# One 512-column matmul in place of two of 260, token halves of 256 and 264, and the low weight products last

## The chip, the cores and the metric

The kernel runs on one core of a Trainium2 chip. The metric is the device time of one launch in microseconds; of the kernel before, three runs gave a median of 1429.27 us (1426.93 to 1429.67).

## The reference

Two layers of a decoder trunk, one inference step for 512 prompt tokens and 8 sample tokens that share all weights (520 tokens, model width 1024). What is computed, cut to the frame:

```
for layer in (0, 1):
    z = x @ w_in                              # even: 3592 columns, odd: 2236 columns
    y = mixer(z)                              # even: gated convolution + mLSTM; odd: NSA + DSA attention
    x = layer_norm(ALPHA * x + y @ w_out)
    x = layer_norm(ALPHA * x + square(relu(x @ w_up)) @ w_down)      # 1024 -> 4096 -> 1024
```

All values are float32. Nearly all arithmetic lies in the projections `x @ w`, and these are what the change touches.

## The kernel before, in words

Tokens lie along the free axis: `xT` is held as 8 blocks (k = 0..7) of 128 channels by 520 tokens. A "tile" g is one output block of 128 channels of a projection. There are 191 tiles: 29 of the even input projection (`G_IN0`), 8 of its output projection (`G_OUT0`), 64 of the first MLP (`G_MLP0`: four chunks of 8 up tiles and 8 down tiles), 18 of the odd input projection (`G_IN1`), 8 of its output (`G_OUT1`), 64 of the second MLP (`G_MLP1`).

Operands are split for accuracy: weights into a high part (`wr`, or a part of `ring_lo` in the even projection) and a low part (`ring_lo`), activations into a high part (`xh`, `hh`) and a low part (`xl`, `hl`). A tile is the sum over k of three products: high weight by high activation, high weight by low activation, low weight by high activation. Tokens are cut into two halves of 260 (`H2`), each accumulated in a PSUM bank of its own (`psA(g)`, `psB(g)`), so a tile takes 8 x 3 x 2 = 48 matmuls of 260 columns, all recorded at L1024 (`split_pass`). Two pairs of banks alternate between tiles (`banks_free` waits until the tile two before has been read out).

The order is written out by hand for every engine, with semaphores. Around the MLPs it is:

- PE: an up tile or down tile after the other (`split_tile`). The first 8 up tiles after a norm are a `head`: all 8 tiles over token half 0 first (a half tile of 24 matmuls each), then half 1 of the first four interleaved, then half 1 of the other four. This lets half 0 start while the other engines still norm half 1. The last tiles before a norm are a `tail`, with all half 0 before all half 1.
- ACT, in `hidden`: relu of half 0 out of PSUM (L1636, signals `free_a`), then the high part of the weights four tiles ahead (`w_hi_ahead`, L1599), then the square that makes `hh` (L1643).
- DVE, in `hidden`: relu of half 1 out of PSUM (L1996, signals `free_b`), the low part of the weights four tiles ahead (`w_lo_ahead`, L1972; it waits for the high part), then `hl` (L2001). Down tiles are added to `xT` by DVE, one operation for each half (`residual`, L1983 and L1984). In the head, DVE's and ACT's lists also hold the second half of the norm: DVE `normed` (L2051) and `x_low` (L2068, L2070), ACT `scaled` (L1670).
- POOL squares the relu (L842) and in the head subtracts the mean (`centre`, L808).

In the even input projection, ACT copies half 0 and DVE half 1 out of PSUM (L2291); DVE also runs the convolution and the sample heads there, and the sigmoid's reciprocal (L2310).

Of the kernel before, what the change touches and what calls it, by code (L numbers as in the profile page):

```python
# [27 lines left out]
P = 128  # L28
# [5 lines left out]
H2 = T // 2  # L34
# [43 lines left out]
def build(nc, x_prompt, x_sample, state_conv, state_C, state_n, state_m, cache_kv, cache_idx, cache_win, page_table,  # L78
# [20 lines left out]
    with ExitStack() as ctx:  # L99
# [11 lines left out]
        with ExitStack() as mixer:  # L111
            big = mixer.enter_context(nc.sbuf_tensor("big", [P, KF, T], F32))
            ymix = mixer.enter_context(nc.sbuf_tensor("ymix", [P, KD, T], F32))
            cbuf = mixer.enter_context(nc.sbuf_tensor("cbuf", [P, 4096], F32))
        with ExitStack() as odd:

            odd.enter_context(nc.sbuf_tensor("projections", [P, len(O_NAMES) * T], F32))
            xl1 = odd.enter_context(nc.sbuf_tensor("xl1", [P, KD, T], F32R))
            odd.enter_context(nc.sbuf_tensor("behind", [P, (KF - KD - len(O_NAMES)) * T], F32))
            xh1 = odd.enter_context(nc.sbuf_tensor("xh1", [P, KD, T], F32R))  # L120


        xh = sb("xh", [P, KD, T], F32R)
        xl = sb("xl", [P, KD, T], F32R)
        hh = sb("hh", [P, KD, T], F32R)
        hl = sb("hl", [P, KD, T], F32R)
# [12 lines left out]
        def piece(n):  # L139
# [13 lines left out]
            pn_ok dsd_ev pb_mm pb_ev pt_mm pt_ev kc_ok pc_mm vf_mm vf_ev pc_n pct_mm q_sc q_mm kv_out  # L153
# [248 lines left out]

        def cols(half):
            return slice(half * H2, (half + 1) * H2)

# [14 lines left out]
        def hid_event(c, j, half=None):  # L420

            return j + KD * half if c == 0 else KD * (c + 1) + j

# [87 lines left out]
        XL = {0: xl, 1: xl1, 2: xl}  # L511
        racc = att[:, 0:T]
# [220 lines left out]
        def _(pool):  # L733
# [98 lines left out]
            def hidden(layer, g, c, j, half=None):  # L832
# [3 lines left out]
                if half != 1:  # L836
                    pool.wait_ge(sm["free_a"], g + 1)
# [22 lines left out]
            for k in range(KD):  # L860
                if k not in XE_DVE:
                    pool.wait_ge(sm["tin_a"], k + 2)
                    pool.wait_ge(sm["tin_b"], 1)
                    pool.tensor_tensor(hl[:, k, :], xT[:, k, :], xh1[:, k, :].bitcast(F32), ALU.subtract).then_inc(sm["xe_p"], 1)
# [114 lines left out]
        def _(pe):  # L979
# [32 lines left out]
            def split_pass(gs, halves, hi, lo, ready_hi=None, ready_lo=None, between=None, ks=range(KD)):  # L1012

                for g in gs:
                    weights_here(g)
                for k in ks:
                    for part, ready, x in ((0, ready_hi, hi), (0, ready_lo, lo), (1, None, hi)):
                        if ready:
                            ready(k)
                        first, final = k == ks[0] and x is hi and part == 0, k == ks[-1] and part == 1  # L1020
                        for g in gs:
                            w = w_split(split_of[g])[part]
                            for half in halves:
                                last = pe.matmul(bank(g, half)[0:width(g), 0:H2], w[:, k, :], x[:, k, cols(half)],  # L1024
                                                 start=first, stop=final)
                                if final:
                                    half_done(last, half)
# [3 lines left out]
            def split_tile(g, hi, lo, ready=None, between=None):  # L1031

                banks_free(g)
                split_pass((g,), (0, 1), hi, lo, ready, between=between)
# [14 lines left out]
            def head(n_ln, g):  # L1049
# [10 lines left out]
                for i in range(n):  # L1060
                    if i >= 4:
                        pe.wait_ge(sm["free_a"], g + i - 3)
                    split_pass((g + i,), (0,), XH[n_ln], XL[n_ln], first_tile if i == 0 else None,
# [4 lines left out]
                split_pass(range(g, g + first), (1,), XH[n_ln], XL[n_ln], x_hi_here(n_ln, 1), x_lo_here(n_ln, 1))  # L1068
                for i in range(first, n):
                    if i >= 4:  # L1070
                        pe.wait_ge(sm["free_b"], g + i - 3)
                    split_pass((g + i,), (1,), XH[n_ln], XL[n_ln])

            def tail(n_ln, g, hi, lo, ready=None, ready_b=None, ks=range(KD)):

                for half in range(2):
                    for i in range(TAILS[g]):
                        if half == 0 and i < 2 and n_ln in (0, 2):
                            if i == 1:
                                pe.wait_ge(sm["free_a"], g - 1)  # L1080
                                pe.wait_ge(sm["free_b"], g - 1)
                                split_pass((g, g + 1), (0,), hi, lo, ready, ks=ks)
# [10 lines left out]
                        split_pass((g + i,), (half,), hi, lo, (ready, ready_b)[half] if i == 0 else None, ks=ks)  # L1093
# [31 lines left out]
            def mlp(layer, g):  # L1125

                for c in range(NFC):
                    if c == 0:
                        head(2 * layer, g)
                    else:  # L1130
                        for j in range(KD):
                            split_tile(g + j, xh, xl)
                    g += KD
                    if c < NFC - 1:
                        for j in range(KD):
                            split_tile(g + j, hh, hl, hidden_here(layer, c) if j == 0 else None)
                    else:
                        for j in range(KD - TAILS[TAIL_OF[layer]]):
                            split_tile(g + j, hh, hl, hidden_here(layer, c) if j == 0 else None)
                        tail(2 * layer + 1, TAIL_OF[layer], hh, hl, hidden_here(layer, c))  # L1140
                    g += KD

            def norm_sums(n_ln, half):
# [3 lines left out]
                mm(ps[4 * half][:, 0:H2], meanM[:, :], racc[:, cols(half)])  # L1147
                mm(ps[4 * half + 1][:, 0:H2], meanM[:, :], sacc[:, cols(half)]).then_inc(sm["stats_mm"], 1)
# [34 lines left out]
            split_pass((G_IN0,), (0, 1), xh1, hl, xe_here, xe_low_here)  # L1183
# [6 lines left out]
            for idx in range(len(E_TILE)):  # L1190
                if idx:
                    split_tile(G_IN0 + idx, xh1, hl)
# [5 lines left out]
                if idx == 2:  # L1198
# [4 lines left out]
                    for half in range(2):  # L1203
                        last = mm(ps[4 + half][0:4, 0:H2], ident[0:8, 4:8], gz[:, half * H2:(half + 1) * H2])
# [96 lines left out]
            tail(0, G_OUT0, xh, xl, y_even_here)  # L1301
# [8 lines left out]
            for idx, name in enumerate(O_NAMES):  # L1310
                if idx == 0:
                    head(1, G_IN1)
                if idx >= 4:
                    split_tile(G_IN1 + idx, xh1, xl1, between=selected if idx == 4 else None)
# [263 lines left out]
            tail(2, G_OUT1, xh, xl, y_odd_here(0), y_odd_here(1), Y_ODD)  # L1578
# [15 lines left out]
        def _(act):  # L1594
# [32 lines left out]
            def hidden(layer, g, c, j, half=None):  # L1627
# [3 lines left out]
                if half != 1:  # L1631
                    tile_done(g, 0)
# [3 lines left out]
                    act.activation(rel[j % 2][:, 0:H2], psA(g)[:, 0:H2], ACT.Relu).then_inc(sm["free_a"], 1)  # L1636
# [1102 lines left out]
```

## Time and profile before

| | |
|---|---|
| median of three runs | 1429.27 us |
| span of the profiled execution | 1421.2 us |
| what lies between the two (median less span) | 8.1 us |
| PE busy | 1366.7 us, 96% of the span |
| DVE / ACT / POOL busy | 52% / 36% / 28% |

The page gives the profiled execution as its span, from first to last instruction; it has no time of its own beside it, so the 8.1 us in the table also hold the difference between one execution and a median. In a timeline, the first two numbers of a row are start and duration in us; the duration of a matmul runs into that of the next ones, so that what one costs is read as the distance of starts. A float32 matmul that is not split stands in the trace as two records, a float32r matmul (L1024) as one.

### The profile page before, as it was taken

To read this page: it belongs to the slowest core of one execution; us is meant where nothing else is said; L and a number is where in the kernel's file an instruction comes from. 1 tells how busy PE (TensorE), PEld (TensorE's weight loads), DVE (VectorE), ACT (ScalarE), POOL (GpSimd) and SP (SyncE) were. 2 spreads that over 40 slices of the span, in tenths; PEclk is the share of its full clock that TensorE was granted. 3 is DMA by queue.
4 is the path that set the end of the run, shared out by engine and by line. 5 is a ranking of instruction groups with operands and counts; after the bars stand their busy time and mean duration, and the time that the engine had idled before them with its cause. 6 is when DMAs were issued, how large, how long until landed. Compare 5 with 4: busy or idle time off the path is not lost. (4 is left out here: it accounts for less than half of the span.)

```text
span 1421.2 us, 27641 instructions
## 1 busy us (share of the span) xinstructions
PE 1366.7 (96%) x11359; PEld 1287.3 (91%) x11359; DVE 745.3 (52%) x1378; ACT 504.6 (36%) x1004; POOL 397.1 (28%) x470
## 2 busy tenths in 40 slices
PE   6999998999999999999899999999999999999996
PEld 5999975899999999999899966667999999999996
DVE  3424777667434343343879856454774343343435
ACT  3321224345314023032542366786553032140311
POOL 3014423365101010014744473023652010010102
PEclk9999999999999999999999999999999999999998
DMA  5343170030323131312323226204113313132301
GB/s 156 125 114 107 43 238 6 3 119 31 126 83 117 63 119 60 119 60 52 60 90 60 64 82 216 61 2 120 64 56 120 119 60 119 60 119 69 110 31 60
DMA packets 87196, 123.86 MB, mean 87 GB/s; under 512 B 24438, under 2 KB 42302, under 8 KB 87040
## 3 DMA queue, kind: packets, MB, share of 16 engines
q1 hardware_dynamic: 82048, 107.00, 23.6%
q0 software_dynamic: 5024, 15.10, 3.6%
q8 instruction: 91, 1.49, 0.4%
q14 instruction: 33, 0.27, 0.1%
HBM read 115.62 MB, written 8.57 MB: 87 GB/s over the span
## 5 line engine op out<-in xcount | busy, mean ns | idle before, releaser
L1024 PE MATMUL ps<-xh,ring_lo 128*128 128x260 f32 (+2 forms) x2496 | 503.5, 283 | 1.4 <-ACT big L1599 1.4
L1024 PEld LDWEIGHTS ps<-xh,ring_lo 128*128 128x128 f32 (+2 forms) x2496 | 382.6, 187 | 3.3 <-ACT big L1599 2.3
L1024 PE MATMUL ps<-xl,wr 128*128 128x260 f32 x1568 | 351.4, 283 | 6.1 <-DVE xl L2070 3.9
L1024 PE MATMUL ps<-xh,wr 128*128 128x260 f32 x1568 | 352.9, 284 | 2.5 <-POOL xl L824 1.2
L1024 PEld LDWEIGHTS ps<-xl,wr 128*128 128x128 f32 x1568 | 255.2, 188 | 8.2 <-DVE xl L2070 5.1
L1024 PEld LDWEIGHTS ps<-xh,wr 128*128 128x128 f32 x1568 | 256.0, 188 | 5.0 <-ACT att L1636 1.4
L842 POOL TENSOR_TENSOR att<-att 128x520 f32<-128x520 f32 (+1 forms) x80 | 77.3, 967 | 548.6 <-DVE att L1996 521.5
L1972 DVE TENSOR_TENSOR ring_lo<-ring,wr 128x1024 fp32r<-128x1024 f32 (+1 forms) x144 | 192.1, 1337 | 62.1 <-ACT wr L1599 62.0
L1024 PE MATMUL ps<-hh,wr 128*128 128x260 f32 x1024 | 222.1, 283 | 0.0
L1024 PE MATMUL ps<-hh,ring_lo 128*128 128x260 f32 x1024 | 221.8, 283 | 0.0
L1024 PE MATMUL ps<-hl,wr 128*128 128x260 f32 x1024 | 221.7, 283 | 0.0
L1599 ACT ACTIVATE wr<-ring 128x1024 fp32r<-128x1024 f32 (+1 forms) x162 | 167.4, 1049 | 130.1 <-PE ps L1024 120.4
L1024 PEld LDWEIGHTS ps<-hh,wr 128*128 128x128 f32 x1024 | 164.5, 188 | 0.2 <-issue 0.2
L1024 PEld LDWEIGHTS ps<-hh,ring_lo 128*128 128x128 f32 x1024 | 164.5, 188 | 0.0
L1024 PEld LDWEIGHTS ps<-hl,wr 128*128 128x128 f32 x1024 | 164.0, 188 | 0.0
L1636 ACT ACTIVATE att<-ps 128x260 f32<-128x260 f32 x64 | 24.6, 384 | 304.4 <-PE ps L1024 304.4
L1983 DVE TENSOR_TENSOR xT<-xT,ps 128x260 f32<-128x260 f32 x96 | 37.5, 422 | 162.9 <-PE ps L1024 162.9
L1996 DVE TENSOR_SCALAR att<-ps 128x260 f32<-128x260 f32 x64 | 27.4, 428 | 137.4 <-PE ps L1024 137.4
L1024 PE MATMUL ps<-hl,ring_lo 128*128 128x260 f32 (+1 forms) x464 | 93.4, 283 | 0.0
L1599 ACT ACTIVATE big<-ps 128x260 f32<-128x260 f32 (+6 forms) x104 | 40.3, 402 | 148.5 <-PE ps L1024 133.2
L789 POOL TENSOR_TENSOR ring_lo<-ring,wr 128x1024 fp32r<-128x1024 f32 x18 | 43.3, 2412 | 109.8 <-ACT wr L1599 109.8
L986 PE MATMUL ps<-big 128*64 128x128 f32 (+3 forms) x504 | 66.7, 348 | 4.8 <-DVE small L2694 3.3
(354 smaller groups left out, 1620.8 us busy)
## 6 DMA issues: line engine op xcount, KB each, us to landing
ring<-in_w_up SPq DMA_DIRECT2D x16, 2048.0 KB, 7.9
ring<-in_w_down SPq DMA_DIRECT2D x16, 2048.0 KB, 7.9
ring<-in_w_in_e SPq DMA_DIRECT2D x9, 1024.0 KB, 5.6
ring<-in_w_in_e SPq DMA_DIRECT2D x2, 2048.0 KB, 8.8
ring<-in_w_out_e SPq DMA_DIRECT2D x2, 2048.0 KB, 8.8
ring<-in_w_in_o SPq DMA_DIRECT2D x16, 256.0 KB, 5.0
ring<-in_cache_kv POOLq DMA_DIRECT2D x32, 128.0 KB, 2.4
ring<-in_w_out_o SPq DMA_DIRECT2D x8, 512.0 KB, 8.9
```

What stands on the lines that cost most here:

```text
L789: pool.tensor_tensor(w_l, w_raw(u), w_h.bitcast(F32), ALU.subtract).then_inc(sm["w_lo_p"], 1)
L842: pool.tensor_tensor(hid[j % 2][:, cc], rel[j % 2][:, cc], rel[j % 2][:, cc], ALU.mult).then_inc(sm["hid_sq"], 1)
L986: return pe.matmul(out, lhsT, rhs, start=start, stop=stop, skip_group_check=True)
L1024: last = pe.matmul(bank(g, half)[0:width(g), 0:H2], w[:, k, :], x[:, k, cols(half)], start=first, stop=final)
L1599: return act.activation(out, in_, ACT.Copy, scale=scale)
L1636: act.activation(rel[j % 2][:, 0:H2], psA(g)[:, 0:H2], ACT.Relu).then_inc(sm["free_a"], 1)
L1972: dve.tensor_tensor(w_l, w_raw(u), w_h.bitcast(F32), ALU.subtract).then_inc(sm["w_lo"], 1)
L1983: last = (dve.tensor_tensor(x, x, y, ALU.add) if scale is None else dve.scalar_tensor_tensor(x, x, scale, y, ALU.mult, ALU.add))
L1996: dve.tensor_scalar(rel[j % 2][:, H2:T], psB(g)[:, 0:H2], 0.0, None, ALU.max).then_inc(sm["free_b"], 1)
```

## The change

Tokens are halved as 256 and 264. In most tiles (`apart`: all output and MLP tiles but the first tile of each MLP, and 23 of the 29 even input tiles; 165 tiles in all) the bank of half 0 is used as two regions of 256 columns. One matmul of 512 columns multiplies the high weights with the high and the low activations of half 0 at once (high activations into one region, low activations into the other); the low-weight product is added to the second region. Whoever reads half 0 out adds the two regions. To have high and low activations in one access pattern, they are put into one tensor (`x2`, `h2`, `x12`, `xe2`). Tiles that wait for nothing at their start (`low_last`) run all 8 k of the high weights first and wait for the low weights only then. DVE and ACT swap their halves in the even projection and in `hidden`.

```diff
+HALVES = (slice(0, 256), slice(256, T))
+HW = (256, T - 256)
...
+        def apart(g, half):
+            if half or g in (G_IN0, G_IN0 + GATE, G_MLP0, G_MLP1) or G_IN1 <= g < G_OUT1:
+                return False
+            return g >= G_OUT0 or not 16 <= E_TILE[g - G_IN0] < 20
...
+            def product(g, half, part, n, k, x, order, first, final):
+                hi, lo = order
+                w = w_split(split_of[g])[part][:, k, :]
+                m = HW[half]
+                region = bank(g, half)[0:width(g), :]
+                last = None
+                if not apart(g, half):
+                    last = pe.matmul(region[:, 0:m], w, x[:, n, k, cols(half)], start=first and n == hi, stop=final)
+                elif part:
+                    last = pe.matmul(region[:, m:2 * m], w, x[:, hi, k, cols(half)], start=False, stop=final)
+                elif n == lo:
+                    both = region.rearrange("p (n t) -> p n t", n=2)
+                    last = pe.matmul(both if hi == 0 else both[:, ::-1], w, x[:, :, k, cols(half)], start=first, stop=False)
+                if final:
+                    half_done(last, half)
...
+            def low_last(g, x, order, between=None):
+                pe.wait_ge(sm["w_hi"], split_of[g] + 1)
+                for k in range(KD):
+                    for n in order:
+                        for half in range(2):
+                            product(g, half, 0, n, k, x, order, k == 0, False)
...
+                weights_here(g)
+                for k in range(KD):
+                    for half in range(2):
+                        product(g, half, 1, order[0], k, x, order, False, k == KD - 1)
...
@@ ACT, hidden @@
-                if half != 1:
-                    tile_done(g, 0)
+                if half != 0:
+                    tile_done(g)
+                    act.wait_ge(sm["free_b"], g)
...
-                    act.activation(rel[j % 2][:, 0:H2], psA(g)[:, 0:H2], ACT.Relu).then_inc(sm["free_a"], 1)
+                    act.activation(rel[j % 2][:, cols(1)], psB(g)[:, 0:HW[1]], ACT.Relu).then_inc(sm["free_b"], 1)
+                if half != 1:
+                    act.wait_ge(sm["free_a"], g + 1)
+                    act.activation(rel[j % 2][:, cols(0)], rel[j % 2][:, cols(0)], ACT.Relu).then_inc(sm["rel_ok"], 1)
                 if g + 1 != TAIL_OF[1]:
                     w_hi_ahead(g, 1 if half is None else half)
...
@@ DVE @@
+                if apart(g0 + m, half):
+                    link(last)
+                    last = dve.tensor_tensor(x, x, bank(g0 + m, half)[:, HW[half]:2 * HW[half]], ALU.add)
...
+            def summed(out, g, n=P):
+                if apart(g, 0):
+                    return dve.tensor_reduce(out, psA(g)[0:n, :].rearrange("p (n t) -> p t n", n=2), AX.X, ALU.add)
+                return dve.tensor_copy(out, psA(g)[0:n, 0:HW[0]])
...
-                if half != 0:
-                    tile_done(g)
+                if half != 1:
+                    tile_done(g, 0)
...
-                    dve.tensor_scalar(rel[j % 2][:, H2:T], psB(g)[:, 0:H2], 0.0, None, ALU.max).then_inc(sm["free_b"], 1)
+                    summed(rel[j % 2][:, cols(0)], g).then_inc(sm["free_a"], 1)
                 if g + 1 != TAIL_OF[1]:
                     w_lo_ahead(g, 1 if half is None else half)
```

How the instructions of PE stand in an up tile of the steady part, before (one k, halves in banks `ps0` and `ps1`):

```order
L1024 MATMUL ps0<-xh,ring_lo 128x260
L1024 MATMUL ps1<-xh,ring_lo 128x260
L1024 MATMUL ps0<-xh,wr 128x260
L1024 MATMUL ps1<-xh,wr 128x260
L1024 MATMUL ps0<-xl,wr 128x260
L1024 MATMUL ps1<-xl,wr 128x260
```

and after:

```order
L1041 MATMUL ps0<-x2,wr 128x512
L1036 MATMUL ps1<-x2,wr 128x264 x2
L1041 MATMUL ps0<-x2,wr 128x512
L1036 MATMUL ps1<-x2,wr 128x264
L1038 MATMUL ps0<-x2,ring_lo 128x256
L1036 MATMUL ps1<-x2,ring_lo 128x264
L1038 MATMUL ps0<-x2,ring_lo 128x256
L1036 MATMUL ps1<-x2,ring_lo 128x264
```

(the last two k of the high weights and the first two of the low). Two matmuls of `ps0` in a k have become one; the low-weight products (`ring_lo`) have gone behind all eight k.

ACT at the start of the first MLP's head, before; L1636 is the relu out of PSUM, L1599 `wr<-ring` the high part of weights, L1643 the square:

```order
L1677 ACTIVATE att<-ps 128x260
L1636 ACTIVATE att<-ps 128x260 [waits mm_a]
L1599 ACTIVATE wr<-ring 128x1024 [waits mm_b,w_slot0]
L1643 ACTIVATE hh<-att 128x260 [waits free_a]
L1681 ACTIVATE att<-att 128x260 [waits std_in]
L1636 ACTIVATE att<-ps 128x260 [waits mm_a]
L1599 ACTIVATE wr<-ring 128x1024 [waits mm_b,w_slot0]
```

and after, with the relu at L1686 and the high part at L1645:

```order
L1727 ACTIVATE att<-ps 128x264
L1686 ACTIVATE att<-att 128x256 [waits free_a]
L1645 ACTIVATE wr<-ring 128x1024 [waits mm_b,w_slot0]
L1693 ACTIVATE h<-att 128x256 [waits rel_ok]
L1731 ACTIVATE att<-att 128x264 [waits std_in]
L1686 ACTIVATE att<-att 128x256 [waits free_a]
L1645 ACTIVATE wr<-ring 128x1024 [waits mm_b,w_slot0]
```

The relu's wait has changed from `mm_a` (signalled by PE) to `free_a` (now signalled by DVE), and it stands ahead of the weights' high part as before.

DVE in the same head, before; `ring_lo<-ring,wr` is the low part of the weights, L2001 `hl`, L2042 to L2070 the norm of half 1:

```order
L1972 TENSOR_TENSOR ring_lo<-ring,wr 128x8x128
L2001 TENSOR_TENSOR hl<-att,hh 128x260
L2042 RECIPROCAL att<-att 128x260
L2051 TENSOR_TENSOR xT<-xT,att 128x260 x2
L1972 TENSOR_TENSOR ring_lo<-ring,wr 128x8x128
L2001 TENSOR_TENSOR hl<-att,hh 128x260
```

and after:

```order
L2044 COPY att<-ps 128x256
L2022 TENSOR_TENSOR ring_lo<-ring,wr 128x8x128
L2060 TENSOR_TENSOR h<-att,h 128x256
L2101 RECIPROCAL att<-att 128x264
L2110 TENSOR_TENSOR xT<-xT,att 128x264 x2
L2043 TENSOR_REDUCE att<-ps 128x256
L2022 TENSOR_TENSOR ring_lo<-ring,wr 128x8x128
L2060 TENSOR_TENSOR h<-att,h 128x256
```

DVE's list in the head has one operation more for each half tile, ahead of the weights' low part.

## Rows read from the trace of the kernel before

**Rows 1.** The page: span, and busy time by engine.

```profile
span 1421.2 us, 27641 instructions
...
PE 1366.7 (96%) x11359; PEld 1287.3 (91%) x11359; DVE 745.3 (52%) x1378; ACT 504.6 (36%) x1004; POOL 397.1 (28%) x470
```

**Rows 2.** PE's waits: what it waited for, us in total, times, longest.

```profile
PE ps L1024 <- DVE xl L2070: 3.9, 5, 1.4
PE ps L1024 <- POOL xl L830: 2.3, 2, 1.2
PE ps L1024 <- DVE ring_lo L1972: 1.0, 2, 0.5
```

**Rows 3.** ACT's timeline in a steady up chunk: start, us, operation, idle before.

```profile
1133.12 0.39 ACT L1636 ACTIVATE att<-ps 128x260 f32<-128x260 f32 x1 [27.59 <-PE ps L1024]
...
1173.49 0.39 ACT L1636 ACTIVATE att<-ps 128x260 f32<-128x260 f32 x1 [3.91 <-PE ps L1024]
```

**Rows 4.** PE's timeline in the gate tile (weights of 8 columns).

```profile
26.00 0.63 PE L1024 MATMUL ps<-xh,ring_lo 128*8 128x260 f32 x4
...
30.95 0.64 PE L1024 MATMUL ps<-xh,ring_lo 128*8 128x260 f32 x4
```

**Rows 5.** PE's timeline in the mLSTM: unsplit matmuls, two records each.

```profile
227.32 1.28 PE L986 MATMUL ps<-att 128*128 128x128 f32 x10
228.53 1.03 PE L986 MATMUL ps<-att,small 128*1 128x128 f32 x8
...
250.03 1.02 PE L986 MATMUL ps<-att 128*128 128x512 f32 x2
250.89 0.59 PE L986 MATMUL ps<-big 128*128 128x256 f32 x2
251.32 0.81 PE L986 MATMUL ps<-att,ones 128*128 128x384 f32 x2
```

**Rows 6.** ACT's timeline in the second MLP's head.

```profile
1037.61 0.39 ACT L1636 ACTIVATE att<-ps 128x260 f32<-128x260 f32 x1
1037.87 1.07 ACT L1599 ACTIVATE wr<-ring 128x1024 fp32r<-128x1024 f32 x1
1038.82 0.43 ACT L1643 ACTIVATE hh<-att 128x260 fp32r<-128x260 f32 x1
```

**Rows 7.** DVE's timeline in the same head.

```profile
1038.98 1.61 DVE L1972 TENSOR_TENSOR ring_lo<-ring,wr 128x1024 fp32r<-128x1024 f32 x1
...
1053.43 1.22 DVE L1972 TENSOR_TENSOR ring_lo<-ring,wr 128x1024 fp32r<-128x1024 f32 x1
```

**Rows 8.** PE's timeline in the same head: the last half tile and what follows.

```profile
1054.79 0.36 PE L1024 MATMUL ps<-xh,wr 128*128 128x260 f32 x1 [0.51 <-DVE ring_lo L1972]
...
1057.74 0.64 PE L1024 MATMUL ps<-xh,wr 128*128 128x260 f32 x4
```

**Rows 9.** DVE's timeline at the end of the even input projection.

```profile
175.55 0.42 DVE L2291 COPY big<-ps 128x260 f32<-128x260 f32 x1
...
200.00 0.43 DVE L2291 COPY big<-ps 128x260 f32<-128x260 f32 x1
...
205.99 0.68 DVE L2331 COPY att<-ps 128x512 f32<-128x512 f32 x1
206.59 1.15 DVE L2336 TENSOR_TENSOR att<-ps,att 128x512 f32<-128x512 f32 x2
```

**Rows 10.** PE's timeline at the same place.

```profile
207.69 1.12 PE L986 MATMUL ps<-small 4*128 4x512 f32 x2 [2.18 <-POOL att L894]
```

**Rows 11.** DVE's timeline, last up tile and first down tile of a steady chunk.

```profile
1176.23 0.69 DVE L2001 TENSOR_TENSOR hl<-att,hh 128x520 fp32r<-128x520 f32 x1
1179.26 0.76 DVE L1983 TENSOR_TENSOR xT<-xT,ps 128x260 f32<-128x260 f32 x2 [2.34 <-PE ps L1024]
```

**Rows 12.** Two stretches: length, busy PE, PEld, DVE, ACT, POOL, then granted clock, DMA.

```profile
828.00:830.00 2.00, 1.58 (x10) 1.35 (x12) 1.89 (x8) 1.47 (x5) 2.00 (x4) 0.56 0.00 0
205.00:207.00 2.00, 0.51 (x2) 0.00 (x0) 1.86 (x8) 1.20 (x4) 0.00 (x0) 1.00 1.05 404
```

More of the change, by code:

```diff
@@ L33 @@
 T = S + B
-H2 = T // 2
+HALVES = (slice(0, 256), slice(256, T))
+HW = (256, T - 256)
 QT = S // P
@@ L1010, in weights_here, with split_pass @@
                 pe.wait_ge(sm[by], n)
-            def split_pass(gs, halves, hi, lo, ready_hi=None, ready_lo=None, between=None, ks=range(KD)):
+            def product(g, half, part, n, k, x, order, first, final):
[13 more added lines that the diff above has]
+                    half_done(last, half)
+            def split_pass(gs, halves, x, order=(0, 1), ready_hi=None, ready_lo=None, between=None, ks=range(KD)):
+                hi, lo = order
                 for g in gs:
@@ L1016, in split_pass, with split_tile @@
                 for k in ks:
-                    for part, ready, x in ((0, ready_hi, hi), (0, ready_lo, lo), (1, None, hi)):
+                    for part, ready, n in ((0, ready_hi, hi), (0, ready_lo, lo), (1, None, hi)):
                         if ready:
                             ready(k)
-                        first, final = k == ks[0] and x is hi and part == 0, k == ks[-1] and part == 1
                         for g in gs:
-                            w = w_split(split_of[g])[part]
                             for half in halves:
[L1024 to L1027, printed above, removed]
+                                product(g, half, part, n, k, x, order, k == ks[0] and not part, k == ks[-1] and part == 1)
                     if between and k == ks[3]:
                         between()
-            def split_tile(g, hi, lo, ready=None, between=None):
+            def low_last(g, x, order, between=None):
[4 more added lines that the diff above has]
+                            product(g, half, 0, n, k, x, order, k == 0, False)
+                    if between and k == 3:
+                        between()
+                weights_here(g)
+                for k in range(KD):
+                    for half in range(2):
+                        product(g, half, 1, order[0], k, x, order, False, k == KD - 1)
+            def split_tile(g, x, order=(0, 1), ready=None, between=None):
                 banks_free(g)
-                split_pass((g,), (0, 1), hi, lo, ready, between=between)
+                if ready:
+                    split_pass((g,), (0, 1), x, order, ready)
+                else:
+                    low_last(g, x, order, between)
             def x_hi_here(n_ln, half):
@@ L1067, in head @@
                 first = n // 2
-                split_pass(range(g, g + first), (1,), XH[n_ln], XL[n_ln], x_hi_here(n_ln, 1), x_lo_here(n_ln, 1))
+                split_pass(range(g, g + first), (1,), *X[n_ln], x_hi_here(n_ln, 1), x_lo_here(n_ln, 1))
                 for i in range(first, n):
```

106 lines of the change are left out of this document (56 added, 50 removed).

## The prediction

> **What bounds the kernel now.** I read the page's busy times first: PE is busy 96% of the span, the next engine 52% [rows 1]. Then PE's waits: its longest sources among the projections add up to some 7 us [rows 2], so nearly all the time is the stream of projection matmuls. So the price of one matmul decides, and I took it from a stretch without waits: ACT's relu of half 0 comes once a tile, and two that lie seven tiles apart are 40.37 us apart [rows 3], which is 5.767 us for a tile and, over 48 matmuls, 120.1 ns each. At the granted clock of 1.00 (2.4 GHz) 260 columns would stream in 108.3 ns. So 11.8 ns of every matmul are not columns, and the question is whether that charge comes once per instruction or is a floor under short ones.
>
> The trace answers it from the side. In the gate tile the weights have 8 columns instead of 128, and a k of six matmuls takes (30.95 - 26.00) / 7 = 0.707 us, 117.9 ns each [rows 4]: loading fewer weight columns hardly helps. The unsplit matmuls of the mLSTM stand as two records, each with twice its columns to stream. With 128 columns (106.7 ns to stream) a record takes (228.53 - 227.32) / 10 = 121 ns; with 256 columns (213.3 ns) it takes (251.32 - 250.89) / 2 = 215 ns; with 512 (426.7 ns) it takes (250.89 - 250.03) / 2 = 430 ns [rows 5]. The charge is 14 ns at 107 ns of streaming but 2 to 3 ns at 213 ns and above. That is a floor of about 120 ns, not a charge that every instruction pays.
>
> **The change, part by part.**
>
> *Matmuls.* In 165 tiles, each with 8 k, two matmuls of 260 columns become one of 512: 1320 instructions fewer. The columns stay the same (512 + 256 + 3 x 264 = 1560 = 6 x 260). The 512-column matmul was never run in this split form. Its stream of 213.3 ns is that of the 256-column record, so I take 216 ns [rows 5]. The others have 256 or 264 columns, 107 and 110 ns of stream, under the floor: 120 ns as now. A k falls from 6 x 120 to 4 x 120 + 216, by 24 ns; a tile by 0.192 us. Bounds for the 512: 213 ns from below (its columns at full clock, 27 ns saved) and 240 ns from above (two records of the short kind, nothing saved); I take the value of the row with the same stream. The sum for PE alone: 1320 x 24 ns = 31.7 us (4.4 in the even input, 1.5 in each output projection, 12.1 in each MLP).
>
> The Trainium skill (TensorE: Matmul & The Clock Gate, Back-to-back issue gap) gives a lone matmul N/2.4 + 2.5 ns. By it 260 columns would cost 111 ns and joining two would save 2.5 ns, 3.4 us in all; the trace's 120.1 ns disagree with it here [rows 3], and the same section says that pairs of load and matmul are spaced by both.
>
> *Low products last.* `low_last` needs the low weights 8 k later. Only two PE waits, 1.0 us in all, are for them [rows 2], and the larger, 0.51 us, is in a head [rows 8], where `split_pass` still stands. Worth nothing (0 to 0.5 us).
>
> *Readout in the steady MLP.* A down tile costs DVE one more addition on half 0: two now take 0.76 us [rows 11], so about 0.4 us more in a tile of 5.6 us. An up tile: DVE sums two regions (512 elements read). A copy of 512 elements out of PSUM takes 0.60 us from start to start [rows 9], a third of a microsecond more than the 260 of now. The relu of half 0 becomes a third step on ACT, behind DVE. For the last up tile of a chunk the chain is: sum 0.6, relu 0.3, high part 1.0, low part 1.3, `hl` 0.7, so `hl` is done about 4.1 us after half 0 of the tile, against (1176.23 + 0.69) - 1173.49 = 3.4 now [rows 3, 11]. The down tile needs it at its last k, 7 x 0.70 = 4.9 us in. Hidden, with 0.8 us to spare; if DVE runs slower beside POOL, at most some tenths at each of 6 such places.
>
> *The two MLP heads.* Here I expect a large part of the gain to go. DVE is without a pause from 1038 to 1059 us, and the last half tile of token half 0 starts at 1054.79, after waiting 0.51 us for its low weights, which DVE finished at 1053.43 + 1.22 = 1054.65 [rows 7, 8]. DVE makes four such low parts here, one after each hidden tile, with pieces of the norm between. Before, the high part was ready early, because ACT took its relu straight from PE. Now ACT's relu waits for DVE, the high part is queued behind the relu, and DVE's low part waits for the high part: what was parallel becomes a round trip. For the first tile (a copy, no sum): copy 0.35, relu 0.3, high part 0.95 (start to start 1037.87 to 1038.82 [rows 6]), handovers 0.1: the low part starts at about 1040.7 instead of 1038.98 [rows 7], 1.7 us later. For each of the next three: sum 0.6, relu 0.3, high part 0.95, three handovers 0.15: 2.0 us. Together 7.7 us. Against it, DVE's operations are slowed beside POOL now (the same low part takes 1.61 us at 1038.98 and 1.22 at 1053.43 [rows 7]), and some of POOL's work will fall into the new pauses: I take off 1.5 us. So the last half tile starts 6.2 us later than now and, being 0.2 us shorter, half 1 starts (1057.74 now [rows 8]) 6.0 us later. Bounds: 0, if ACT's part hides, and 8 us. The first MLP's head has the same list. In both, the 7 tiles' gain of 1.3 us is not collected either. Loss: 2 x (6.0 + 1.3) = 14.6 us. Half 1 behind it is not late: the normed activations of its last k are needed 8.6 us after its start, and DVE has them after about 5.
>
> *End of the even input projection.* From 175.55 to 206.59 us DVE runs almost without pause, and PE then waits 2.18 us on the chain that leaves it [rows 9, 10]. The last six tiles' faster matmuls bring nothing (6 x 0.19 = 1.1 us) and DVE's six readouts are 0.25 us longer each (1.5 us): 2.6 us.
>
> *Norms.* The last half-0 residual before each of three norms is 0.4 us longer, and PE waits for what comes of it [rows 2]: 1.2 us (0 to 2).
>
> *Sum:* 31.7 - 14.6 - 2.6 - 1.2 = 13.3 us. The profiled span of 1421.2 us would become 1407.9; with the 8.1 us between span and median, 1429.3 becomes 1416.0 us.
>
> **The rivals.**
>
> *The heads cost nothing.* ACT and DVE overlap after all, or PE's slack takes it. For it: ACT itself is idle for long stretches. Against it: PE already waits there [rows 8]. It gives 31.7 - 2.6 - 1.2 = 27.9 us: 1401.4 us.
>
> *The pauses lower the clock.* In the heads PE would stop for 3 us twice. Between 828 and 830 us the granted clock fell to 0.56 (towards 1.2 GHz) after PE had stood for 1.9 us; between 205 and 207 us PE was busy only 0.51 of 2 us and the clock stayed at 1.00 [rows 12]. The first speaks for it, the second against. A stretch at half clock of some 7 us, as that one was, costs up to 3.5 us in each head: 1423 us.
>
> *A charge per instruction.* If the 11.8 ns are paid once by each instruction whatever its length, the 512 costs 225 ns and a k saves some 12 ns. Of the 165 tiles 145 collect it (not those of the heads and the last six), 1160 k x 12 = 14 us, and the losses that remain are 2 x 6.0 + 1.5 + 1.2 = 14.7 us: 1430 us. Against it stand [rows 5].
>
> *Slower: the joined matmul is no cheaper than two.* It reads two runs of 256 activations that lie 16 KB apart, and in the even input writes them in reversed order. If that costs 240 ns, nothing is gained and 14.7 us are lost: 1444 us. The point from which this decides is 227 ns for the 512-column matmul (240 - 14.7 us / 1160). For it: no row shows such a matmul. Against it: each run is 1 KB long, and the 2 x 256 columns lie side by side in PSUM. The Trainium skill (PSUM — Partial Sum Buffer, Specifications (TRN2)) states that "any non-contiguous AP slows matmuls significantly"; by that rule this rival would hold for the reversed writes at least, but no row here shows it.
>
> **How the numbers follow.** Forecast 0.48 at 1416 (its own range 1410 to 1422); heads free or half free 0.17 at 1401; clock 0.15 at 1423; charge per instruction 0.10 at 1430; slower 0.10 at 1444. 0.2% (2.9 us) is about what can be told from no change. Faster than 1426.4: 0.48 + 0.17 + most of 0.15 = 0.78. Within 0.2%: most of the 0.10 at 1430 = 0.09. Slower: 0.13. The range 1400 to 1432 leaves out the 0.10 at 1444 and a few hundredths below.
>
> **What would show it.** In the profile after: starts of a 512-column matmul and the next 216 ns apart, others 120; tile distance in a steady chunk 5.58 us; PE busy near 1335 us. In both heads: DVE idle before its low parts, with ACT's high part as releaser, about 1.3 us each, four times; PE waits for `ring_lo` of 1 to 3.5 us, 6 to 8 us in a head. PE's waits in steady chunks: none. The forecast fails if the 512 costs 227 ns or more, if heads show no such wait, or if the last `hl` of a chunk makes PE wait at each down chunk.

## The result, and the profile after

The changed kernel took 1437.47 us (median of 4 runs, 1436.85 to 1440.07), the kernel before 1428.76 us (median of 4): a ratio of 1.0073, 95% interval [1.0053, 1.0094]. It is 8.7 us slower. Forecast were 1416 us and 13 us faster; the time lies above the range of 1400 to 1432.

The page after, span and busy times, then two of its groups (busy us, mean ns of one | idle before, and what ended it):

```profile
span 1436.3 us, 25213 instructions
...
PE 1370.6 (95%) x10039; PEld 1230.3 (86%) x10039; DVE 788.3 (55%) x1458; ACT 531.1 (37%) x1068; POOL 395.0 (27%) x470
...
L1041 PE MATMUL ps<-x,wr 128*128 128x512 f32 x624 | 240.6, 403 | 10.6 <-DVE ring_lo L2022 9.3
L2022 DVE TENSOR_TENSOR ring_lo<-ring,wr 128x1024 fp32r<-128x1024 f32 (+1 forms) x144 | 181.3, 1262 | 105.1 <-ACT wr L1645 104.9
```

PE issues 1320 matmuls fewer and is busy for longer (1366.7 us before [rows 1]). The instructions are gone, the time is not.

PE's waits after (total, times, longest):

```profile
PE ps L1041 <- DVE ring_lo L2022: 9.3, 5, 3.7
...
PE ps L1036 <- DVE x L2129: 3.7, 5, 1.4
...
PE ps L1002 <- DVE big L2043: 2.1, 1, 2.1
PE ps L1002 <- POOL att L817: 2.1, 4, 0.9
```

Waits for the low weights were 1.0 us before [rows 2] and are 9.3 now. That is one term. The second is the price of a matmul. PE's timeline in a steady up tile, from its first matmul to its first low-weight product:

```profile
1161.53 0.28 PE L1036 MATMUL ps<-x,wr 128*128 128x264 f32 x1
1161.65 0.39 PE L1041 MATMUL ps<-x,wr 128*128 128x512 f32 x1
...
1164.97 0.40 PE L1041 MATMUL ps<-x,wr 128*128 128x512 f32 x1
1165.20 0.28 PE L1036 MATMUL ps<-x,wr 128*128 128x264 f32 x1
1165.32 0.28 PE L1038 MATMUL ps<-x,ring_lo 128*128 128x256 f32 x1
```

Between the first and the last 512-column matmul lie seven steps of one 512 and two 264s: 3.32 us, 0.474 each. Less 2 x 0.120 for the 264s this leaves 0.234 us for the 512, where the forecast had 0.216. ACT's readout of half 1 gives the tile as a whole, six tiles apart:

```profile
1150.31 0.39 ACT L1683 ACTIVATE att<-ps 128x264 f32<-128x264 f32 x1 [27.41 <-PE ps L1036]
...
1184.55 0.39 ACT L1683 ACTIVATE att<-ps 128x264 f32<-128x264 f32 x1 [3.21 <-PE ps L1036]
```

34.24 / 6 = 5.707 us a tile, against 5.767 [rows 3]: 0.060 us gained, not 0.192; over 165 tiles 9.9 us, not 31.7.

The third term shows in the head. The second MLP's head on PE:

```profile
1047.75 0.59 PE L1041 MATMUL ps<-x,wr 128*128 128x512 f32 x1
...
1060.05 0.47 PE L1041 MATMUL ps<-x,wr 128*128 128x512 f32 x1 [0.72 <-DVE ring_lo L2022]
...
1066.79 0.77 PE L1041 MATMUL ps<-x,wr 128*128 128x512 f32 x1 [3.71 <-DVE ring_lo L2022]
...
1067.57 0.63 PE L1041 MATMUL ps<-x,wr 128*128 128x512 f32 x1
1068.00 0.41 PE L1038 MATMUL ps<-x,ring_lo 128*128 128x256 f32 x1
1068.21 0.63 PE L1041 MATMUL ps<-x,wr 128*128 128x512 f32 x1
...
1075.09 1.12 PE L1036 MATMUL ps<-x,wr 128*128 128x264 f32 x8
```

The same head before began at

```profile
1036.66 0.48 PE L1024 MATMUL ps<-xh,wr 128*128 128x260 f32 x1
```

so that from the head's first matmul to half 1 (1057.74 before [rows 8], 1075.09 after) lie 27.34 us in place of 21.08. On DVE, the sum (L2043), the pause for ACT and the low part (L2022) stand in a row:

```profile
1056.28 0.68 DVE L2043 TENSOR_REDUCE att<-ps 128x256 f32<-128x512 f32 x1
1058.40 1.50 DVE L2022 TENSOR_TENSOR ring_lo<-ring,wr 128x1024 fp32r<-128x1024 f32 x1 [1.44 <-ACT wr L1645]
...
1063.31 0.68 DVE L2043 TENSOR_REDUCE att<-ps 128x256 f32<-128x512 f32 x1
1065.42 1.23 DVE L2022 TENSOR_TENSOR ring_lo<-ring,wr 128x1024 fp32r<-128x1024 f32 x1 [1.43 <-ACT wr L1645]
```

DVE idles 1.4 us for each low part, and PE waits 0.72 and 3.71 us. After the long wait a k step takes 0.64 us (1067.57 to 1068.21) in place of some 0.35. The windows say why (length, busy PE, PEld, DVE, ACT, POOL, then granted clock, DMA share, GB/s):

```profile
1064.00:1066.00 2.00, 0.00 (x0) 0.00 (x0) 0.58 (x1) 1.97 (x4) 0.61 (x1) 0.87 0.00 0
1066.00:1068.00 2.00, 1.21 (x4) 1.04 (x5) 2.00 (x5) 1.41 (x3) 0.00 (x0) 0.50 0.00 0
1068.00:1070.00 2.00, 2.00 (x8) 1.71 (x7) 1.03 (x2) 0.90 (x2) 0.41 (x1) 0.50 0.00 0
1070.00:1072.00 2.00, 2.00 (x8) 1.55 (x6) 1.51 (x2) 1.93 (x5) 0.91 (x2) 0.50 0.00 0
1072.00:1074.00 2.00, 2.00 (x12) 1.67 (x11) 1.97 (x6) 0.55 (x1) 0.00 (x0) 0.92 0.04 12
```

The granted clock fell from 2.4 to 1.2 GHz while PE stood, and stayed there for 5.5 us of full work after the wait (1066.79 to some 1072.3). At half clock the 512 takes 0.43 us (1067.57 to 1068.00) and a k 0.64 in place of 0.353, so each microsecond of it loses 0.45: 2.5 us here. The first MLP's head does the same (waits of 0.72 and 3.72 us; half clock from 338.4 to 345.3 us, of which 5.2 us are work after the wait: 2.3 us lost).

**The bill** for the two profiled executions, 1436.3 less 1421.2 = 15.1 us: tiles -9.9; waits for low weights +8.3; half clock behind them in the two heads +4.8; the norm's wait (POOL att L817, 0.2 before) +1.9; end of the even input projection +3.3 (the mLSTM behind it is 1.9 us later, although the 23 joined tiles ahead of it had gained 1.4). Half clock elsewhere is an estimate, since PE often waits in the mixers anyway: it stood at half clock from 823 to 837 and from 704 to 707 us, before only from 828 to 835, 10.2 us more, which is at most 4.6 us at 0.45. Together 13.0; 2.1 us are not assigned. These stretches differ between executions of one kernel: in the second profile of the changed kernel (e8_after_again) they stand at 205, 703, 823, 881 and 986 us, and half clock in its first head lasts only 3.4 us, behind the same waits. The profile of before is of one of its fastest executions (clock 0.994, its runs average 0.989 to 0.991), so that the medians lie closer (8.7 us) than these two spans.

### The profile page after: what moved, and what is told of

Its sections match the earlier page's. It is cut to its first block and busy times, and to the rows that moved or that the text cites. A ratio compares the mean times of both kernels' runs of the same rounds, so it can differ in the third digit from the quotient of the medians.

```text
span 1436.3 us, 25213 instructions
## 1 busy us (share of the span) xinstructions
PE 1370.6 (95%) x10039; PEld 1230.3 (86%) x10039; DVE 788.3 (55%) x1458; ACT 531.1 (37%) x1068; POOL 395.0 (27%) x470
## 5 line engine op out<-in xcount | busy, mean ns | idle before, releaser
L1036 PE MATMUL ps<-x,wr 128*128 128x264 f32 (+3 forms) x1888 | 340.4, 285 | 5.7 <-DVE x L2129 3.7
L1036 PEld LDWEIGHTS ps<-x,wr 128*128 128x128 f32 (+1 forms) x1888 | 299.4, 187 | 23.6 <-DVE x L2129 4.8
L1041 PE MATMUL ps<-x,wr 128*128 128x512 f32 x624 | 240.6, 403 | 10.6 <-DVE ring_lo L2022 9.3
L2022 DVE TENSOR_TENSOR ring_lo<-ring,wr 128x1024 fp32r<-128x1024 f32 (+1 forms) x144 | 181.3, 1262 | 105.1 <-ACT wr L1645 104.9
L1036 PE MATMUL ps<-h,wr 128*128 128x264 f32 x1024 | 220.6, 284 | 0.0
L1036 PE MATMUL ps<-x,ring_lo 128*128 128x264 f32 (+3 forms) x944 | 209.5, 283 | 0.0
L1645 ACT ACTIVATE wr<-ring 128x1024 fp32r<-128x1024 f32 (+1 forms) x162 | 167.2, 1047 | 112.0 <-PE ps L1036 97.2
L1041 PE MATMUL ps<-h,wr 128*128 128x512 f32 x512 | 197.7, 394 | 0.6 <-DVE h L2060 0.6
L1036 PEld LDWEIGHTS ps<-h,wr 128*128 128x128 f32 x1024 | 186.0, 188 | 13.7
L1038 PE MATMUL ps<-x,ring_lo 128*128 128x256 f32 x624 | 160.6, 283 | 0.0
L1036 PE MATMUL ps<-xe,ring_lo 128*128 128x264 f32 (+2 forms) x840 | 158.0, 287 | 1.9 <-DVE big L2043 1.9
L1036 PEld LDWEIGHTS ps<-x,ring_lo 128*128 128x128 f32 (+1 forms) x944 | 159.1, 187 | 0.0
L1041 PEld LDWEIGHTS ps<-h,wr 128*128 128x128 f32 x512 | 96.4, 188 | 5.1 <-issue 0.9
```

Of the source, the lines that this page charges most:

```text
L1036: last = pe.matmul(region[:, 0:m], w, x[:, n, k, cols(half)], start=first and n == hi, stop=final)
L1038: last = pe.matmul(region[:, m:2 * m], w, x[:, hi, k, cols(half)], start=False, stop=final)
L1041: last = pe.matmul(both if hi == 0 else both[:, ::-1], w, x[:, :, k, cols(half)], start=first, stop=False)
L1645: return act.activation(out, in_, ACT.Copy, scale=scale)
L2022: dve.tensor_tensor(w_l, w_raw(u), w_h.bitcast(F32), ALU.subtract).then_inc(sm["w_lo"], 1)
```

## The experiments

The theories at the outset. **1**: the heads' round trip (DVE, ACT, DVE) stops PE, and the stop lowers the clock. **2**: the sums of two regions on DVE are what is late. For the matmul, **A**: float32r costs by the column, above 1/2.4 ns, with little for an instruction; **B**: short matmuls have a floor or the two runs of 256 a penalty; **C**: contention with other engines.

"At clock 0.990" in the table compares times without the clock's share. Over 191 runs of this study the time rises by 1.21 us for each 0.001 that the mean granted clock of a run is lower (one slope, fitted within each kernel), and each kernel's mean is moved along it. One run of "the same again", whose recorded clock of 0.942 does not fit its time of 1430.4, is left out of both clock columns. The column also takes out what the half clock in the heads costs, since that is part of a kernel's lower clock. Each kernel was measured beside the kernel before, in one job.

| kernel | median us | ratio to before | mean clock, and of before in the job | us at clock 0.990 |
|---|---|---|---|---|
| before | 1427.6 to 1431.3 | 1 | 0.989 to 0.991 | 1429.0 |
| after | 1437.5 | 1.0073 [1.0053, 1.0094] | 0.986 | 1432.8 |
| after, again | 1440.0 | 1.0085 [1.0054, 1.0115] | 0.985, 0.991 | 1433.3 |
| high part first in heads | 1426.6 | 0.9979 [0.9955, 1.0003] | 0.992, 0.989 | 1427.8 |
| the same again | 1430.3 | 1.0008 [0.9991, 1.0025] | 0.988, 0.990 | 1428.1 |
| none joined | 1434.7 | 1.0043 [1.0015, 1.0070] | 0.988, 0.989 | 1433.7 |
| heads' tiles not joined | 1433.5 | 1.0035 [1.0013, 1.0057] | 0.989, 0.989 | 1432.6 |
| heads as before, input's end not joined | 1428.7 | 1.0006 [0.9989, 1.0022] | 0.987, 0.991 | 1424.4 |
| none joined, high part first | 1427.6 | 1.0004 [0.9983, 1.0025] | 0.989, 0.991 | 1427.4 |
| low products not last | 1437.0 | 1.0062 [1.0039, 1.0084] | 0.986, 0.990 | 1432.1 |
| high part first, input's end not joined | 1429.8 | 0.9993 [0.9974, 1.0012] | 0.989, 0.990 | 1427.4 |
| halves of 256 and 264 alone | 1427.1 | 1.0001 [0.9982, 1.0019] | 0.989, 0.991 | 1426.2 |

**Matmuls by themselves (e1_widths, e5_widths2).** Neither computes anything of the model: after one load, PE alone runs series of 40 or more matmuls, while the other engines rest.

> Only PE works here: runs of 32 matmuls of one kind, one after the other, operands split as in the kernel (float32r) and for contrast bfloat16; nothing of the model is computed and the outputs are left unwritten. Theory A (each column of a float32r matmul costs more than a clock: 0.452 ns a column and 2.5 ns an instruction, from 120.1 ns at 260 columns and 234 ns at 512 in the changed kernel): starts lie apart by 118 ns at 256, 120 at 260, 122 at 264, 133 at 288, 147 at 320, 176 at 384, 205 at 448, 234 at 512 columns, two runs of 256 like 512 in one. Theory B (a floor of 120 ns under short ones, as predicted, and 512 columns in two separate runs cost extra): 120 ns from 256 up to 288, 136 at 320, 163 at 384, 216 at 512 in one run, 234 only with two runs. Theory C (the other engines' traffic slows it in the kernel): without them N/2.4 + 2.5 ns, 111 at 260 and 216 at 512. bfloat16 by A: 111 and 216, since the charge is that of four-byte columns.

All series stood on one source line, so that the trace gives only sums: the pattern 512 + 264 + 264 repeats every 0.475 us, as in the kernel (0.474). C falls; between A and B it tells nothing. The second version gives each width a line:

```
for i in range(40):                                        # one such block for each width N
    pe.matmul(ps[i % 2][:, 0:N], wr[:, i % 8, :], x2[:, 0, i % 8, 0:N], start=True, stop=True)
... # L147: as the changed kernel in the even input, two runs, reversed
    pe.matmul(ps[i % 2][:, 0:512].rearrange("p (n t) -> p n t", n=2)[:, ::-1], wr[:, i % 8, :], x2[:, :, i % 8, 0:256], ...)
```

> PE alone again, forty matmuls of each kind, each kind on a line of its own so that its price can be read; nothing of the model is computed. Theory A (0.452 ns a column and 2.5 ns an instruction for float32r): 60 ns at 128 columns or the floor of weight loads there (about 80 to 120), 118 at 256, 120 at 260, 122 at 264, 133 at 288, 147 at 320, 176 at 384, 205 at 448, 234 at 512; two runs, reversed order, one bank and a weight block used again all without effect. Theory B (floor of 120 and a penalty for two runs): 216 at 512 in one run, 234 in two, 120 up to 288. bfloat16: N/2.4 and about 1 to 2.5 ns.

```profile
126.09 4.93 PE L103 MATMUL ps<-x,wr 128*128 128x260 f32 x40
130.85 9.53 PE L107 MATMUL ps<-x,wr 128*128 128x512 f32 x40
140.22 7.19 PE L111 MATMUL ps<-x,wr 128*128 128x384 f32 x40
147.25 5.00 PE L115 MATMUL ps<-x,wr 128*128 128x264 f32 x40
152.09 4.94 PE L119 MATMUL ps<-x,wr 128*128 128x256 f32 x40
156.86 6.03 PE L123 MATMUL ps<-x,wr 128*128 128x320 f32 x40
162.73 8.25 PE L127 MATMUL ps<-x,wr 128*128 128x448 f32 x40
170.82 5.44 PE L131 MATMUL ps<-x,wr 128*128 128x288 f32 x40
176.10 4.57 PE L135 MATMUL ps<-x,wr 128*128 128x128 f32 x40
180.51 5.40 PE L139 MATMUL ps<-x,wr 128*128 128x64 f32 x40
...
197.51 9.53 PE L147 MATMUL ps<-x,wr 128*128 128x512 f32 x40
206.88 9.53 PE L151 MATMUL ps<-x,wr 128*128 128x512 f32 x40
...
229.66 4.60 PE L163 MATMUL ps<-xb,wb 128*128 128x260 bf16 x40
234.10 4.53 PE L167 MATMUL ps<-xb,wb 128*128 128x256 bf16 x40
```

From start to start, over 40: 128 columns (180.51 - 176.10) / 40 = 110.3 ns, 256 columns 119.2, 260 119.0, 264 121.0, 288 132.0, 320 146.8, 384 175.8, 448 202.3, 512 234.2. From 260 columns up that is 0.458 ns a column (448: 0.451), with next to nothing left for an instruction. 256 columns cost 2 ns more than by this price, and 128 cost 110 ns in place of 59: short matmuls have a bound from below. So A holds: the 120 ns of the kernel before were nearly all columns, and joining two matmuls of 256 saves 2 x 119.2 - 234.2 = 4.2 ns. Whether these 4.2 ns are a charge for an instruction or that bound, which 256 columns would just meet, the series do not decide. B falls: 288 columns cost 132 ns and not 120, and 512 in one run cost 234.2 and not 216; the reversed two-run form (L147) takes (206.88 - 197.51) / 40 = 234.2 ns like the plain one. The same 260 columns in bf16 take (234.10 - 229.66) / 40 = 111.0 ns.

The Trainium skill (TensorE: Matmul & The Clock Gate, Back-to-back issue gap) has N/2.4 + 2.5 ns: 110.8 for 260 columns. The bf16 rows agree with it, the float32r rows do not (119.0; for 512, 216 by the rule, 234.2 measured). By what the Trainium skill states of non-contiguous access patterns in PSUM (PSUM — Partial Sum Buffer, Specifications (TRN2)) the reversed write would be slower; as two regions of 256 columns it is not (234.2 ns). Patterns with shorter pieces were not run.

**High part first in the heads (e2_hi_first, e11_hi_first_again).** ACT makes the weights' high part before its relu, so that it no longer waits for DVE's sum:

```diff
+                if half == 0:
+                    w_hi_ahead(g, 0)
                 if half != 1:
                     act.wait_ge(sm["free_a"], g + 1)
                     act.activation(rel[...], rel[...], ACT.Relu).then_inc(sm["rel_ok"], 1)
-                if g + 1 != TAIL_OF[1]:
+                if g + 1 != TAIL_OF[1] and half != 0:
                     w_hi_ahead(g, 1 if half is None else half)
```

> The changed kernel, but in the two MLP heads ACT makes the weights' high part before its relu of half 0, so that the high part no longer waits for DVE's sum. Theory 1 (round trip: DVE's low parts wait for ACT's high part, which is queued behind a relu that waits for DVE, and the pauses lower the clock): the waits of 0.72 and 3.7 us for ring_lo in each head fall to 0.5 to 1.5 us in all, the half clock in both heads goes, the time falls by 2 x (3 + 3.4) = 13 us from 1437.5 to about 1425. Rival 2 (DVE's extra sums alone make the head late): at most 1 us each is won and the clock still falls: 1435 to 1437.

PE's waits for low weights in it:

```profile
PE ps L1041 <- DVE ring_lo L2024: 5.0, 5, 1.2
```

The longest is 1.2 us in place of 3.7, and in neither head does the clock fall. Moving one instruction in two heads took the ratio from 1.0073 to 0.9979. Theory 1 is shown. Its sizes were too high: waits of 0.5 to 1.5 us were expected and a head still has 2.3 (1.20 and 1.11; 4.4 in the changed kernel, 0.5 before), since DVE's sums stay.

> The kernel with ACT's high part ahead of its relu in the heads, once more with more rounds: 0.9979 if the first measurement stands (0.9968 to 0.9992). If the first one was a lucky chip, 1.000 or above.

The second measurement gave 1.0008, with the same waits and again no half clock in the MLP heads; the changed kernel measured again gave 1.0085. The intervals of the two measurements overlap between 0.9991 and 1.0003: this kernel is no faster than before by anything that I can measure.

**The sums taken out (e4_head_plain, e3_none_joined).** In the first, tiles of the heads are not joined; in the second none is (`apart` returns False always), but ACT and DVE keep the new order.

```diff
-            if half or g in (G_IN0, G_IN0 + GATE, G_MLP0, G_MLP1) or G_IN1 <= g < G_OUT1:
+            if half or g in (G_IN0, G_IN0 + GATE) or G_MLP0 <= g < G_MLP0 + KD or G_MLP1 <= g < G_MLP1 + KD or G_IN1 <= g < G_OUT1:
```

> The changed kernel with no joined matmul in the 16 tiles of the two heads; ACT's relu of half 0 still waits for DVE. Theory 1 (round trip through ACT): DVE's list becomes shorter by 3 x 0.25 us before the last low part, the waits for ring_lo stay at 3 us or more in each head, the clock still falls: 1434 to 1437. Rival 2 (the sums make the head late): the waits fall to under 1 us, 1425.

> The changed kernel with no tile joined: every tile is six matmuls a k (256 and 264 columns), half 0 is copied and not summed; halves, low products last and the swapped roles of ACT and DVE stay. Theory A (512 columns cost 234 ns): each tile costs PE 0.064 us more, 165 tiles 10.6 us, and DVE's sums and double residuals go, which gives back in the heads about 0.6 us a tile of DVE's list. If the heads' round trip stays at three quarters of its size and the clock still falls there: 1437.5 + 10.6 - 4 = 1444. If without the sums the heads no longer lower the clock: 1437. Rival B (the joined matmuls cost more than they save): faster than 1433.

Longest wait for low weights 3.4 us in both, 8.4 and 8.5 us in all, and the clock fell in the heads of both (for 6.8 us in one, 3.4 in the others). The sum makes only 0.3 of the 3.7 us; theory 2 falls as the main cause. The round trip does it even with a plain copy, since ACT's high part is behind DVE either way. The steady tile of e3_none_joined is 5.740 us: of the 0.060 us gained a tile, 0.027 came from cutting 520 into 256 and 264, and 0.033 from joining, which is 8 x 4.2 ns. The expectation of 1444 or 1437 us was a miss (1434.7): it priced joining at 0.064 us a tile, twice too high, and did not count what the new halves bring.

**Both put together (e7_none_hi_first).**

> As the run with the weights' high part ahead of the relu in the heads, and besides no tile joined. Its distance to that run is what the joined matmuls are worth with the heads mended. By the price of 234 ns: 165 x 0.064 = 10.6 us lost, of which DVE's sums at the end of the even input, at the norms and in the heads give back 3 to 5: 6 to 8 us above that run, a ratio to before of 1.002 to 1.004. By the price of 240 or more (nothing won): a ratio of 0.995 to 0.998.

1.0004, so joining on top of it (0.9979, 1.0008) is worth nothing that can be told: 5 us less in tiles (165 x 0.033), less what the sums cost: waits for low weights are 2.7 us here and 5.0 there, and the norms and the end of the even input wait longer there too. The expected 6 to 8 us rested on 0.064 us a tile again.

**Heads as before (e6_both).** ACT takes the relu of half 0 straight from PE's bank in the heads, the heads' tiles are not joined, nor are the last six of the even input:

```diff
                 if half == 0:
+                    tile_done(g, 0)
+                    act.activation(rel[j % 2][:, cols(0)], psA(g)[:, 0:HW[0]], ACT.Relu).then_inc(sm["free_a"], 1)
...
+            if G_IN0 + 23 <= g < G_OUT0:
+                return False
```

> The changed kernel with both heads as before (no joined matmul, ACT's relu of half 0 straight out of PE's bank) and the last six tiles of the even input not joined. If the price of 512 columns is 234 ns and the losses are the heads, the clock in them and the end of the even input: 145 tiles x 0.064 = 9.3 us won, 1.7 lost at the norms, 1421 where before is 1428.8 (ratio 0.9947). If the joined matmuls cost elsewhere what they save: 1427 to 1430.

A miss: 1.0006. The mechanism did as expected (low weights 1.7 and 0.4 us on two lines, no half clock in an MLP head), and at clock 0.990 this is the fastest of all, 4.6 us under before. But its twelve runs had clocks of 0.985 to 0.989, and in the profiled one the clock is halved at 207 to 214, 251 to 255, 698 to 702, 818 to 832 and 838 to 842 us, in and around the mixers.

**The rest (e8 to e10).** The changed kernel again; low products taken k by k as before (`split_pass` in place of `low_last`); high part first with the last six even input tiles not joined.

> The changed kernel itself, beside these runs on the same chip, so that the others can be set against it: a ratio to before of 1.005 to 1.009.

> The changed kernel, except that no tile runs its low-weight products last: every tile takes them k by k, as before the change. If that order did nothing (my reading of the kernel before: only 1.0 us of waits for low weights), this kernel takes what the changed one takes, ratio 1.008 to the kernel before, and the waits in the heads are the same 4.4 us each. If the order was needed, because the joined matmuls leave the low weights less time, PE's waits for ring_lo outside the heads rise from about nothing to several us and the ratio goes above 1.012. If the order itself cost something, the ratio falls below 1.005.

> ACT makes the high part of the weights ahead of its relu in the heads, and the last six tiles of the even input projection are not joined, so that DVE has no sums there. Joined matmuls elsewhere bring (165 - 6 - 14 tiles) x 0.064 us = 9.3 us, norms cost 1.7, the even input's end costs nothing: 7.6 us if the clock stays as in the kernel before, ratio 0.9947. If the clock takes it back as it did in the kernel with the heads of before, the ratio is 0.998 to 1.001 and the mean granted clock lies 0.003 or more below that of the kernel before in the same job.

The changed kernel repeats (1.0085). The order of the low products is worth nothing measurable: 10.2 us of waits for low weights (9.3 and 10.4 in the two profiles of the changed kernel), the same waits in the heads, a steady tile of 5.713 us against 5.707. The third came out at 0.9993 where 0.9947 was expected, and its mean clock was only 0.001 lower. I had left out its waits for low weights: 5.1 us, as in e2_hi_first, against 1.0 before. That takes the 7.6 us down to 3.5; at clock 0.990 it is 1.6 us under before.

**Halves alone (e12_halves_only).** e6_both with `apart` always False.

> No matmul is joined anywhere; what stays of the change is the halving into 256 and 264 tokens, the low products last and the swapped halves outside the heads; the heads take their relu straight from PE's banks as before. In the kernel with no joined matmul the steady tiles were 5.740 us apart, 0.027 less than the 5.767 of before, and in the changed kernel 5.707, so joining alone was worth 0.033 us a tile. If that holds here: 190 tiles x 0.027 = 5.1 us, nothing lost in heads, norms or at the end of the even input, so the span at the clock of before falls by 5 us and the ratio is 0.9965. If this kernel's granted clock is lower too, by some 0.003 as that of the kernel with both repairs (0.987 on average against 0.990), the ratio is 0.999 to 1.001, and joined matmuls are not what lowers it; if its clock is that of before, they are suspected.

```profile
1135.47 0.39 ACT L1683 ACTIVATE att<-ps 128x264 f32<-128x264 f32 x1 [27.58 <-PE ps L1036]
...
1169.91 0.39 ACT L1683 ACTIVATE att<-ps 128x264 f32<-128x264 f32 x1 [3.51 <-PE ps L1036]
```

Six tiles in 34.44 us are again 5.740 each. Ratio 1.0001, clock 0.989 against 0.991, at clock 0.990 2.8 us under before where 5 were worked out. Joining is therefore not the only thing that goes with a lower clock; nor do all versions have one (0.992 against 0.989 in e2_hi_first). No version tried beats the kernel before.

## Why the prediction was wrong, step by step

- **What bounds the kernel: right as far as it went.** PE's stream decides. **The step that failed** is the one after it: it took a column at 1/2.4 ns, so that "11.8 ns of every matmul are not columns", and from two unsplit matmuls' records (215 ns for 256 columns, 121 ns for 128 [rows 5]) it read "a floor of about 120 ns, not a charge that every instruction pays". Those are another kind of matmul. A float32r column costs 0.458 ns: 260 of them make 119 of the 120.1 ns, and joining had next to nothing to save. The 512 costs 234 ns and not 216, past the prediction's own sign of failure at 227; the term of 31.7 us measured 9.9, of which 5.5 (165 x 0.033) by joining and the rest by the new halves, which the forecast had at nothing. This is 21.8 us of the 21.5 between forecast and result; the losses, 18.4 us in the forecast, came to some 17.8 by the terms below.
- **The rival prices.** "A charge per instruction" would save 12 ns a k; 4 were measured, and no run shows that they are such a charge. The slower rival named 227 ns as the point from which it decides, and the price lay beyond it, for a reason that it did not have: neither two runs nor the reversed write cost anything. (The 3.4 us that the prediction gives for a saving of 2.5 ns at each of 1320 joined pairs are 3.3.)
- **Heads: right in place and mechanism; the size was met in part by luck.** Expected were pauses of 1.3 us on DVE and half 1 6.0 us later. Measured: 1.4 us, and half 1 6.3 us later in the second head (27.34 less 21.08). But only 3.9 of it are waits (4.4 less 0.5, where waits of 6 to 8 us were expected); 2.5 are half clock, less 0.4 for the faster half tiles. The half clock was the rival "the pauses lower the clock", priced at up to 3.5 us a head. As that rival was added to the forecast's 6.0, it would have counted some of this twice.
- **Low products last: worth nothing,** as forecast (e9_no_low_last).
- **End of the even input, norms: right, a little low.** The mLSTM's wait of 2.18 us ends 1.9 us later (209.61 against 207.69 [rows 10]), although the tiles before it gained 1.4: a loss of 3.3 us (2.6 forecast). The norms' waits rose by 1.9 (1.2 forecast).

```profile
209.61 1.12 PE L1002 MATMUL ps<-small 4*128 4x512 f32 x2 [2.18 <-POOL att L910]
```

- **Steady readout: nearly free,** as forecast: PE waits 0.6 us once for `h`.
- With measured sizes the prediction's own sum reads 9.9 - 2 x (3.9 + 2.4) - 3.3 - 1.9 = -7.9 us. The medians say -8.7, the two profiled executions -15.1. At equal clock the table has 3.8 us, and without the half clock the terms make 3.1. That sum and medians agree is worth no more than these fractions of a microsecond, since half clock in a head varies between executions (2.8 to 6.0 us of work behind the same wait).

**What stays open:** why runs of one and the same kernel have mean clocks from 0.986 to 0.995 (before: 1434.8 to 1421.0 us), and why several versions lie 0.002 to 0.006 lower than before beside them; in the changed kernel the heads are a part of it. The stretches at half clock stand mostly around 205, 250 and 820 to 840 us, where PE has pauses of its own; that these pauses cause them is not shown. It was not tried to fill these pauses. Also open is why 256 and 264 are cheaper in the kernel than twice 260 (0.6 ns a matmul); e5_widths2, with 119.2 + 121.0 against 2 x 119.0, does not show it.

## What to carry to other kernels

Take the price of a new instruction size from the same data format, or measure it alone first: a series of 40 matmuls would have shown that joining saves 4 ns and not 24. When a helper engine is put between the matrix engine and an engine that also prepares its weights, move the weights' part ahead of the new wait. And count a stop of some microseconds in a dense stream of matmuls twice, as the wait and as the half clock after it: here 3.9 and about 2.4 us a head.

## What the runs showed of the hardware

- float32r matmuls: 110.3 ns at 128 columns, 119.2 at 256, 175.8 at 384, 234.2 at 512, that is 0.458 ns a column from 260 up; at half clock the 512 takes 430 ns (in the head). bf16: 111.0 at 260. Two runs, or two runs written in reverse, cost the same as one.
- The clock can fall while PE is busy without a gap. In e5_widths2, behind series of 40 matmuls with 128 and 64 columns (busy PE, PEld, DVE, POOL, then granted clock, DMA share, GB/s):

```profile
60.00:80.00 20.00, 20.00 (x130) 19.42 (x129) 0.00 (x0) 0.00 (x0) 1.00 0.00 1
80.00:90.00 10.00, 10.00 (x84) 10.00 (x84) 0.00 (x0) 0.00 (x0) 0.93 0.00 0
90.00:100.00 10.00, 10.00 (x37) 8.24 (x37) 0.00 (x0) 0.00 (x0) 0.73 0.01 2
```

- Waits of 3.4 to 3.7 us in the MLP heads went with 2.8 to 6.0 us of work at half clock during or behind them (the changed kernel, e3, e4, e8, e9); with waits of at most 1.2 us there the clock stayed (e2, e6, e7, e10, e11, e12).
